# VectorE makes one of GpSimd's weight low parts: slab 147, the second of the wide projection hv

## What is computed

```
z = u @ w_in[i]
zq, zkv, zg, zc, zm = jnp.split(z, IN_SPLITS, axis=-1)
kc = compress(kv[0], cmp_pos_k[i], w_cmp_k1[i], w_cmp_k2[i])
vc = compress(kv[1], cmp_pos_v[i], w_cmp_v1[i], w_cmp_v2[i])
c = c_val * jax.nn.sigmoid(c_gate)
c = causal_dwconv(c, conv_w[i], conv_b[i])
ga, gb = jnp.split(jax.nn.sigmoid(zm), 2, axis=-1)

def compress(kv, pos, w1, w2):
    blocks = kv[:, :, idx] + pos
    return jax.nn.gelu(flat @ w1) @ w2
```

## Time and profile before

| | |
|---|---|
| Median of three runs | 868.77 us (868.51, 868.77, 870.84) |
| The profiled execution | 868.49 us |
| Its span | 866.7 us |
| TensorE (PE) busy | 848.3 us, 98% |
| GpSimd (POOL) busy | 628.6 us, 73% |
| VectorE (DVE) busy | 556.5 us, 64% |
| ScalarE (ACT) busy | 485.7 us, 56% |

### The profile page before, as it was taken

The page is one execution under the profiler, slowest core; times in us unless marked ns, Lnnn a source line. Parts: engine busy times, 40 slices in busy tenths (PEclk is TensorE's granted clock), DMA queues, the critical chain, the costliest instruction groups (busy, mean ns, idle before and its releaser), DMA issues.

```text
span 866.7 us, 18295 instructions
## 1 busy us (share of the span) xinstructions
PE 848.3 (98%) x7055; PEld 816.1 (94%) x7055; DVE 556.5 (64%) x1541; ACT 485.7 (56%) x924; POOL 628.6 (73%) x282
## 2 busy tenths in 40 slices
PE   8999999999999999999999999999999999999995
PEld 8999988889998899999999998988999999999995
DVE  5997757783243567677458998875566776641164
ACT  6755476664446456563846457875654444554361
POOL 4999756655997456563879799554868888889681
PEclk9999999999999999999999999999999999999997
DMA  8677633332765343433565567434656666667511
GB/s 327 197 217 218 192 98 99 98 98 76 221 216 161 109 146 102 143 104 116 161 204 184 175 200 226 139 84 120 191 146 190 188 185 185 190 188 219 178 49 50
DMA packets 38678, 138.46 MB, mean 160 GB/s; under 512 B 4416, under 2 KB 4544, under 8 KB 38592
## 3 DMA queue, kind: packets, MB, share of 16 engines
q1 hardware_dynamic: 38592, 137.30, 51.6%
HBM read 136.23 MB, written 1.05 MB: 158 GB/s over the span
## 4 chain that ended last, share of the span: by engine, by line
PE 76%; POOL 4%; DVE 3%; ACT 2%; issue 2%; POOLq 0%; ACTq 0%; DVEq 0%
PE ps L623 21%; PE ps L624 21%; PE ps L625 21%; POOL wl L568 4%; PE ps L845 1%; PE ps L751 1%; PE ps L668 1%; ACT wh L1117 1%; PE ps L650 1%; PE ps L978 1%; PE ps L869 1%; PE ps L841 1%; PE ps L816 1%; PE ps L733 1%; DVE mzb L1900 1%
## 5 line engine op out<-in xcount | busy, mean ns | idle before, releaser
L568 POOL TENSOR_TENSOR wl<-raw,wh 128x1024 fp32r<-128x1024 f32 x254 | 611.4, 2434 | 196.5 <-ACT wh L1117 196.3
L623 PE MATMUL ps<-uh,wh 128*128 128x256 f32 (+1 forms) x1248 | 352.4, 282 | 3.0 <-DVE wl L1647 1.5
L625 PE MATMUL ps<-uh,wl 128*128 128x256 f32 (+1 forms) x1248 | 348.6, 279 | 0.0
L624 PE MATMUL ps<-ul,wh 128*128 128x256 f32 (+1 forms) x1248 | 348.4, 279 | 0.0
L1117 ACT ACTIVATE wh<-raw 128x1024 fp32r<-128x1024 f32 (+1 forms) x256 | 263.7, 1052 | 83.6 <-PE ps L625 81.5
L623 PEld LDWEIGHTS ps<-uh,wh 128*128 128x128 f32 (+1 forms) x1248 | 233.4, 187 | 5.4 <-issue 1.9
L624 PEld LDWEIGHTS ps<-ul,wh 128*128 128x128 f32 (+1 forms) x1248 | 233.9, 187 | 0.0
L625 PEld LDWEIGHTS ps<-uh,wl 128*128 128x128 f32 (+1 forms) x1248 | 233.4, 187 | 0.1
L1801 DVE TENSOR_TENSOR h<-ps,h 128x256 f32<-128x256 f32 x32 | 13.6, 424 | 106.3 <-PE ps L625 106.2
L625 PE MATMUL ps<-ffh,wl 128*128 128x256 f32 x176 | 49.3, 280 | 0.0
L623 PE MATMUL ps<-ffh,wh 128*128 128x256 f32 x176 | 49.1, 279 | 0.0
(11 more groups left out here) (360 smaller groups left out, 1720.4 us busy)
## 6 DMA issues: line engine op xcount, KB each, us to landing
raw<-slabs SPq DMA_DIRECT2D x255, 512.0 KB, 4.0
h<-x_fm SPq DMA_DIRECT2D x4, 256.0 KB, 4.4
out_fm<-outb SPq DMA_DIRECT2D x4, 256.0 KB, 2.2
cst<-shape_consts SPq DMA_DIRECT2D x1, 768.0 KB, 8.7
vec<-vectors SPq DMA_DIRECT2D x1, 299.5 KB, 8.5
pin<-p_fm SPq DMA_DIRECT2D x1, 256.0 KB, 5.6
raw<-slabs SPq DMA_DIRECT2D x1, 128.0 KB, 2.4
vec<-vectors SPq DMA_DIRECT2D x1, 4.0 KB, 2.4
```

The source lines that it names most:

```text
L568: nc.gpsimd.tensor_tensor(wl[:, s % PART_RING, :], raw[:, s % RAW_RING, :], wh[:, s % PART_RING, :].bitcast(f32), ALU.subtract).then_inc(s ...
L623: nc.tensor.matmul(res, w_h, a_h, start=first, stop=False)
L624: nc.tensor.matmul(res, w_h, a_l, start=False, stop=False)
L625: ins = nc.tensor.matmul(res, w_l, a_h, start=False, stop=last)
```

## The change

Slab 147, the second of hv, gets its low part from VectorE, which makes it after it has taken mg9 and ahead of the next six conv steps. GpSimd's loop leaves that slab out. As `wl_ready` now counts one less from there on, and the two engines can finish out of order, a new semaphore `wl_dve` tells of slab 147; who waits for a later slab waits for both.

```
+        dve_low = jobs["hv"].slab0 + 1
+
+        def wait_low(eng, s):
+
+            if s < 0:
+                return
+            if s >= dve_low:
+                eng.wait_ge(sem("wl_dve"), 1)
+            if s != dve_low:
+                eng.wait_ge(sem("wl_ready"), s + (s < dve_low))
...
-                wait(sp_, "wl_ready", s - RAW_RING + 1)
+                wait_low(sp_, s - RAW_RING)
...
             for s in range(FIRST_SLABS, n_slabs):
-
+                if s == dve_low:
+                    continue
                 pool.wait_ge(sem("wh_ready"), s + 1)
...
-                        pe.wait_ge(sem("wl_ready"), s + 1)
+                        wait_low(pe, s)
...
             for n in GATES_BEFORE[1:3]:
                 take_gate(n)
+                if n == GATES_BEFORE[1]:
+                    dve.wait_ge(sem("wh_ready"), dve_low + 1)
+                    tt(wl[:, dve_low % PART_RING, :], raw[:, dve_low % RAW_RING, :],
+                       wh[:, dve_low % PART_RING, :].bitcast(f32), ALU.subtract).then_inc(sem("wl_dve"), 1)
                 conv31(6)
```

## The result

| | median | runs |
|---|---|---|
| before | 868.77 us | 5 runs, 868.47 to 870.84 |
| after the change | 872.81 us | 5 runs, 872.28 to 873.63 |

The ratio is 1.004, with a 95% interval from 1.0027 to 1.0052, that is 2.3 to 4.5 us: the kernel has become slower, by 4.0 us if the medians are compared. The forecast was 1.7 us slower, 870.4, with a range up to 872.6. The profiled execution took 872.57 us with a span of 870.8.

A forecast was written before the change was run, and what follows sets the result against it. TensorE was taken to bound the kernel overall, GpSimd the changed stretch, VectorE close behind. 868.49 us profiled plus 1.7 of VectorE delay gave 870.2, or 870.5 from the median; forecast 870.4, range 868.9 to 872.6.

The forecast's parts named there:

- VectorE is second on the path: Before mg1, VectorE runs a quarter of a microsecond behind GpSimd, so its added work makes mg1 start 1.7 us later.
- What the two engines do to each other: At slab 146, VectorE's operation waits for GpSimd's running one, then works 1.08 us; VectorE goes on 2.17 us later.
- The rival that they don't touch: VectorE's operation at slab 147 is not held up by GpSimd: delay 0.7 us, time 869.2 to 869.5; chance 0.10.
- GpSimd's gain: Low parts of slabs 148 to 151 end 1.4 us earlier; TensorE's gain is lost waiting before mg1.
- The double waits cost nothing: TensorE's second slab wait from slab 148 on is hidden by the queue that runs ahead, costing nothing.
- The clock: Rival: TensorE's thin stretch, 525.8 to 530.6, halves its clock, costing 1.7 to 3.5 us, together 871.9 to 874.0; chance 0.08.
- the third wait: Rival: a third semaphore wait at the start of 108 slabs on TensorE is not hidden, 2.2 us, 872.6; chance 0.06.
- Nothing later gives the time back: From mg1 on, the chain runs through VectorE, ScalarE and TensorE alike, so the 1.7 us stay at every later place.

The follow-up runs named there:

- e2_no_low: The change without its VectorE operation: nobody makes slab 147's low part, VectorE only passes the semaphore on; 871.37 us, ratio 1.0026 to the kernel before.
- e3_dve_only: The kernel before plus a VectorE operation of the same width at the change's place, GpSimd keeping all low parts; 870.50 us, ratio 1.0012.
- e8_after_again: The changed kernel itself, unaltered, measured again on a chip with widely spread times; 874.19 us beside 871.01 for the kernel before, ratio 1.0041.
- the filled kernels: Two runs of the change plus eleven matmuls of ones before ck and three between cv and mg1; 873.51 us beside 871.01, 871.08 beside 869.30.
- e1_fill: The change plus nine matmuls of ones on TensorE between mg0 and ck; 871.84 us, ratio 1.0032 to the kernel before.
- e10_two_steps_only: The change with two conv steps ahead of VectorE's low part and four behind it; 871.07 us beside 869.30 for the kernel before, ratio 1.0017.

## Why the prediction was right and wrong

**VectorE is second on the path.** Right, and the heart of it. mg9 to mg1 grew by 1.72 us, forecast 1.72; with the cost taken away (e2_no_low) it shrank by 0.33, forecast 0.3; with the relief taken away (e3_dve_only) it grew by 1.67. That the changed kernel itself hits 1.72 is helped by luck: ck and cv ran at half the clock there and ended at the very moment at which VectorE let mg1 go. In e8_after_again they ended later, and it was 1.9.

**What the two engines do to each other.** Right, and now shown: VectorE waits until GpSimd's running instruction has ended, works for 1.08 us after that, and GpSimd's next one takes 3.38 us. The forecast had 2.25 and 3.4 us for these two. The rival that they don't touch is out. The Trainium skill's GPSIMD Engine Reference, section Key points, is borne out in its sentence on contention; its factor of two for VectorE held for the work itself (1.22 us beside GpSimd's 2.42), but not for the 2.34 us that VectorE paid.

**GpSimd's gain.** Right: slab 148 no longer waited for, mg11 1.36 us closer to mg9, all of it lost before ck, where TensorE idled for 2.23 us. (The prediction's 528.25 for the end of hgl adds up to 528.21; nothing hangs on it.)

**The double waits cost nothing.** Right as far as it can be told: less than 0.2 us of growth over the last 88 slabs, and 1.8 to 2.1 us in all with the gaps filled.

**The clock.** Here the prediction failed. Its sum had no term for the clock: the fall was listed as a rival, with its place (525.8 to 530.6), its price (1.7 to 3.5 us, 871.9 to 874.0 in all) and a chance of 0.08. It came, and from mg1 to mg2 it cost 2.15 us, more than VectorE's delay. The reasons against it were weak. One was that ck and cv split the stretch; but the prediction itself had TensorE idle for some 2.4 and 0.9 of these 4.8 us. The other was that the clock line has its top digit everywhere but in the last slice; but between its first 13 us and that slice the old kernel has no stop longer than 0.77 us, so it had never been put to the test. The one row that showed a fall had a thin stretch before it. The Trainium skill's page TensorE: Matmul & The Clock Gate, section Why this matters for your kernels, asks that long idle gaps between bursts of matmuls be avoided; the gap here, 2.23 us, is shorter than the one that its table names, and the clock fell all the same. The chance should have been the larger one.

The price was a little off as well. Half of the 6.8 us for which the low level lasted would be 3.4 us, but the first 2.0 of them, up to 530.24, fell on ck and cv, where TensorE would have waited for VectorE anyway. The range has its top, 872.6, from the third wait, which cost nothing, and from the cheap end of the clock case; the median lies 0.2 above it. That it is so close is no merit of the forecast 870.4. A ratio of 1.004 means slower by over 0.3%, which had been given 0.14.

**"Nothing later gives the time back".** Right, with 0.4 us of scattered losses up to ya0 that I can't assign; e3_dve_only and the filled kernels show 0.2 to 0.4 of the same.

## What to carry to other kernels

When work is moved from the engine that a path waits for, look at the engine that would be waited for next: if it is a quarter of a microsecond behind and gets the work, the relief is lost and the cost remains. Relief ahead of a fixed wait also widens TensorE's idle gap there, so price the clock with it; leaving work out altogether made this kernel 2 us slower. An instruction with two SBUF inputs on VectorE beside a GpSimd that never rests should be counted with what is left of GpSimd's running instruction, as the three starts measured here show, and put where little of it is left.

## What the runs showed of the hardware

- The granted clock fell without any long stop. In e1_fill it came after 5.5 us in which TensorE was busy for 4.32, with stops of 0.44 and 0.74 us; in e3_dve_only, with 4.22 busy out of 5.0 and one stop of 0.75 us, it did not. What makes the difference was not tried.
- The low stretches of the profiled executions lasted 6.8 or 3.4 us. In e10_two_steps_only the slower executions had the lower mean clocks: 869.6 us at 0.995, 873.0 at 0.990.
- A VectorE operation that waits for GpSimd's instruction is recorded as running: the same 128 x 1024 subtraction stands at 1.22, 1.46, 2.34 and 3.21 us. A mean over such rows says little of the operation.
